# Half of the first norm's modulation columns as products on TensorE, and a new order of the head projections

## What is computed

```python
mod = jax.nn.silu(c) @ w_ada[l] + b_ada[l]            # c: 1 x 1024, w_ada: 1024 x 6144
sh1, sc1, g1, sh2, sc2, g2 = jnp.split(mod, 6, axis=-1)
h = rms_norm(x, g_mix_norm[l]) * (1.0 + sc1[:, None]) + sh1[:, None]
proj = h @ w_in[l]
q_lat, kv_lat, k_pe, qd, kd, vd = jnp.split(proj, SPLITS, axis=-1)
# q, kv from normed q_lat, kv_lat; per-head rms norms; rope on q_pe, k_pe, qd, kd
# two attentions of 8 heads (dense causal; dilated), then
x = x + g1[:, None] * mix                              # mix = both attentions @ w_o
h2 = rms_norm(x, g_ffn_norm[l]) * (1.0 + sc2[:, None]) + sh2[:, None]
x = x + g2[:, None] * (conv-gated ffn of h2)
```

## Time and profile before

| what | value |
|---|---|
| median of 3 runs | 1995.4 us (1995.07 to 1996.27) |
| the profiled execution | 1996.96 us; span from first to last instruction 1995.2 us |
| mean granted TensorE clock | 0.955 |
| PE, DVE, ACT, POOL busy | 93%, 55%, 37%, 14% of the span |
| matmul instructions on PE | 12441 |
| chain that ended last | PE 86%, DVE 6%, ACT 4%, DMA 2% |

### The profile page before, as it was taken

The page is one execution under the profiler, slowest core; times in us unless marked ns, Lnnn a source line. Parts: engine busy times, 40 slices in busy tenths (PEclk is TensorE's granted clock), DMA queues, the critical chain, the costliest instruction groups (busy, mean ns, idle before and its releaser), DMA issues.

```text
span 1995.2 us, 31747 instructions
## 1 busy us (share of the span) xinstructions
PE 1850.2 (93%) x12441; PEld 1631.5 (82%) x12441; DVE 1098.3 (55%) x1742; ACT 744.8 (37%) x1069; POOL 281.0 (14%) x289
## 2 busy tenths in 40 slices
PE   2688779998999999899999999999999899999997
PEld 2565555566888888789999999999999799999995
DVE  5653426556766377754855384433654466654632
ACT  3264436415533233332322263324522454322313
POOL 1001108513000000503004323320000000000000
PEclk8798899989999999989999999998999899999998
DMA  5461320164333332244434462222443123332321
GB/s 182 157 158 45 114 74 12 45 188 86 92 98 90 100 89 88 77 116 123 137 98 99 119 207 70 76 81 92 124 133 99 44 84 93 94 91 81 96 81 46
DMA packets 320275, 198.38 MB, mean 99 GB/s; under 512 B 51159, under 2 KB 303702, under 8 KB 320166
## 3 DMA queue, kind: packets, MB, share of 16 engines
q1 hardware_dynamic: 303520, 154.63, 27.2%
q0 software_dynamic: 9104, 29.02, 4.9%
q10 hardware_dynamic: 7542, 13.23, 1.8%
HBM read 177.23 MB, written 17.24 MB: 97 GB/s over the span
## 4 chain that ended last, share of the span: by engine, by line
PE 86%; DVE 6%; ACT 4%; DMA 2%; issue 2%; SPq 0%; DVEq 0%; POOL 0%; ACTq 0%; POOLq 0%
PE ps L1234 65%; PE ps L1623 3%; PE ps L1682 1%; PE ps L1701 1%; PE ps L1281 1%; DMA ring<-in_w_ada_dram 1%; DVE acol L1842 1%; PE ps L1346 1%; PE ps L1441 1%; PE ps L1476 1%; PE ps L1460 1%; PE ps L1607 1%; PE ps L1603 1%; PE ps L1359 1%; PE ps L1591 1%
## 5 line engine op out<-in xcount | busy, mean ns | idle before, releaser
L1234 PE MATMUL ps<-zhi,whi 128*128 128x264 f32 (+1 forms) x2168 | 685.2, 316 | 23.4 <-DVE zlo L1780 20.2
L1234 PE MATMUL ps<-zhi,wlo 128*128 128x264 f32 (+1 forms) x2168 | 673.8, 311 | 0.0
L1234 PE MATMUL ps<-zlo,whi 128*128 128x264 f32 (+1 forms) x2168 | 672.5, 310 | 0.0
L1234 PEld LDWEIGHTS ps<-zhi,whi 128*128 128x128 f32 x2168 | 415.7, 192 | 56.1 <-issue 24.1
L1770 DVE TENSOR_TENSOR wlo<-stage,whi 128x1024 fp32r<-128x1024 f32 x256 | 327.7, 1282 | 227.3 <-ACT whi L784 221.7
L1234 PEld LDWEIGHTS ps<-zlo,whi 128*128 128x128 f32 x2168 | 416.4, 192 | 22.0 <-issue 2.9
L1234 PEld LDWEIGHTS ps<-zhi,wlo 128*128 128x128 f32 x2168 | 415.6, 192 | 19.3
L784 ACT ACTIVATE whi<-stage 128x1024 fp32r<-128x1024 f32 x256 | 269.2, 1054 | 344.1 <-PE ps L1234 282.0
L1234 PE MATMUL ps<-ghi,whi 128*128 128x264 f32 (+1 forms) x528 | 169.8, 322 | 0.0
L1234 PE MATMUL ps<-ghi,wlo 128*128 128x264 f32 (+1 forms) x528 | 169.7, 321 | 0.0
L1234 PE MATMUL ps<-glo,whi 128*128 128x264 f32 (+1 forms) x528 | 169.6, 321 | 0.0
(11 more groups left out here) (365 smaller groups left out, 2805.7 us busy)
## 6 DMA issues: line engine op xcount, KB each, us to landing
stage<-in_w_up_dram SPq DMA_DIRECT2D x88, 512.0 KB, 3.8
stage<-in_w_in_dram SPq DMA_DIRECT2D x74, 512.0 KB, 4.1
ring<-in_w_ada_dram POOLq DMA_DIRECT2D x32, 512.0 KB, 4.6
stage<-in_w_down_dram SPq DMA_DIRECT2D x32, 512.0 KB, 3.7
adab<-in_w_ada_dram SPq DMA_DIRECT2D x16, 512.0 KB, 7.9
stage<-in_w_down_dram SPq DMA_DIRECT2D x16, 384.0 KB, 3.3
stage<-in_w_o_dram SPq DMA_DIRECT2D x8, 512.0 KB, 3.8
stage<-in_ssm_w_glu_dram SPq DMA_DIRECT2D x8, 512.0 KB, 3.8
```

Of the source, the lines that this page charges most:

```text
L1234: last = pe.matmul(out, w(a, k), x(k, t0, t1), start=(k == 0 and a is whi and x is x_hi), stop=(k == ks - 1 and a is wlo))
```

## The change

- `block` and `block_sums`: DVE multiplies and adds only k = 0 to 3 of each kind (`column`); for k = 4 to 7 PE multiplies the `adab` pieces as stationary operand by the column of `csil`, adding in PSUM, and closes with the ones column on `acol`. Two `acol` sets instead of four.
- DVE, not ACT, copies the transposed x out, one column step of round 0 after each copy. The tables move behind the first products.
- Loads on SP: ada 0 to 3 ahead of `ql` 0 and 1, `ql` 2 ahead of ada 8, `ql` 3 ahead of ada 12. Splits 0 and 1 come before round 1; `first_products` takes three jobs, `ql` 3 becomes a plain job.
- Order of projections: `dk` directly behind `dq`, then `qp`, `kpe`, `kn`, `qn`; groups renumbered. `group_scale` becomes `group_log` and `group_exp` with copy-outs between them.
- Sum 2 moves behind `qn23`, sum 3 behind `dv`, sum 4 from `wo` 4 to `wo` 6, sum 5 behind the norm's statistics; four `asum` tiles.
- The first three splits of `wo` move into attention steps 6 to 8.

The diff, cut to its core (tile addresses, and lists that only follow the new order, are left out):

```diff
-    p.shared("qp", 1, 2, 8)
     p.shared("kn", 1, 4, 8)
-    p.gemm("dk", 4)
     p.shared("qn01", 1, 2, 8)
     p.shared("qn23", 1, 2, 8)
...
             load_unit(sp, 0, unit_views("ql", 0))
             load_unit(sp, 1, unit_views("ql", 1))
-            for u in range(8):
+            for u in range(4, 8):
                 ada_block(u)
             load_unit(sp, 2, unit_views("ql", 2))
+            for u in range(8, 12):
+                ada_block(u)
             load_unit(sp, 3, unit_views("ql", 3))
-            for u in range(8, 16):
+            for u in range(12, 16):
                 ada_block(u)
             sp.dma_start(cst[:, 3 * P:], A["consts"][:, 3 * P:]).then_inc(s_cst2, 16)
             n = 4
-            for name, count in (("kvl", 2), ("dq", 4), ("kpe", 1), ("qp", 1), ("kn", 1), ("dk", 4), ("qn01", 1),
-                                ("qn23", 1), ("mv", 1), ("dv", 4)):
...
-            for k in range(KD):
-                act.wait_ge(xt_mm, k + 1)
-                act.activation(xT[:, k, META:T2], ps[:, 5 + k % 2, :], ACT.Copy).then_inc(xt_done, 1)
+            split_hi(0)
+            split_hi(1)
             act.wait_ge(rs_mm, 1)
             act.activation(rs[:, 0:T1], ps[:, 3, :], ACT.Copy).then_inc(rs_done, 1)
-            for u in range(4):
-                split_hi(u)
+            split_hi(2)
 
             def ahead(name, j):
 
...
-                link(act.activation(sqg[g % 2][:, 0:n, :], ps[:, 4:4 + n, :], ACT.Ln, scale=1.0 / s["w"], bias=small[:, 0:1]))
+                act.activation(sqg[g % 2][:, 0:n, :], ps[:, 4:4 + n, :], ACT.Ln, scale=1.0 / s["w"], bias=small[:, 0:1])\
+                    .then_inc(gln_done, 1)
+
+            def group_exp(g):
+                n = len(GROUPS[g]["tiles"])
+                act.wait_ge(gln_done, g + 1)
                 act.activation(sqg[g % 2][:, 0:n, :], sqg[g % 2][:, 0:n, :], ACT.Exp, scale=-0.5).then_inc(grs_done, 1)
...
             raw("dq", 3)
             act.wait_ge(tab_ready, 2)
             act.activation(tab[:, :, :], tab[:, :, :], ACT.Sin).then_inc(tab_done, 1)
-            raw("kpe", 0)
-            group_scale(0)
-            for j in range(2):
-                raw("qp", j)
-            for j in range(4):
-                raw("kn", j)
-            group_scale(1)
             raw("dk", 0)
             raw("dk", 1)
+            group_log(0)
             raw("dk", 2)
-            group_scale(2)
+            group_exp(0)
             raw("dk", 3)
+            raw("qp", 0)
+            ahead("kpe", 0)
+            group_log(1)
+            raw("qp", 1)
+            group_exp(1)
+            raw("kpe", 0, False)
+            raw("kn", 0)
+            raw("kn", 1)
+            group_log(2)
+            raw("kn", 2)
+            group_exp(2)
+            raw("kn", 3)
             raw("qn01", 0)
-            group_scale(3)
+            group_log(3)
             raw("qn01", 1)
+            group_exp(3)
             raw("qn23", 0)
             raw("qn23", 1)
...
-            for j in range(QB):
-                value_out("mv", j, Vm)
-            group_scale(4)
+            value_out("mv", 0, Vm)
+            value_out("mv", 1, Vm)
+            group_log(4)
+            value_out("mv", 2, Vm)
+            group_exp(4)
+            value_out("mv", 3, Vm)
             for j in range(QB):
                 value_out("dv", j, Vd)
-
-            for u in range(U["wo"], U["wo"] + 3):
-                split_hi(u)
 
...
             for t in range(NS + 5):
+                if 6 <= t < 9:
+                    split_hi(U["wo"] + t - 6)
...
-                pe.wait_ge(acol_done, 2 * r + 2)
+                pe.wait_ge(acol_done, 2 * r + 2)
                 for kind in range(2):
+                    u = 4 * r + 2 * kind + 1
+                    pe.wait_ge(bulk_in[u % 8], 16 * (u // 8 + 1))
                     for i in range(2):
-                        mm = pe.matmul(ps[:, 4 + r, 2 * i + kind:2 * i + kind + 1], acol[2 * r + kind][:, i * P:(i + 1) * P],
-                                       const("ones", n=1), start=True, stop=True)
+                        o = ps[:, 4 + r, 2 * i + kind:2 * i + kind + 1]
+                        for k in range(4):
+                            pe.matmul(o, adab[u % NADA][:, k, i * P:(i + 1) * P], csil[:, 4 + k:5 + k], start=k == 0, stop=False)
+                        mm = pe.matmul(o, acol[2 * (r % 2) + kind][:, i * P:(i + 1) * P], const("ones", n=1),
+                                       start=False, stop=True)
                 mm.then_inc(mod_mm, 1)
...
-                for j in range(4):
+                for j in range(3):
...
             block_sums(0)
+            pe.wait_ge(diag_done, 1)
+            for t in range(QB):
+                mm = pe.matmul(ps[:, 3, t * P:(t + 1) * P], const("ones"), diag[:, t, :], start=True, stop=True)
+            mm.then_inc(rs_mm, 1)
             block_sums(1)
             for k in range(KD):
                 first_products(k)
-                if k in (0, 3):
-                    block_sums(2 + k // 3)
...
                 pe.wait_ge(ada_done, KD * (g - 1))
                 if g > 2:
                     pe.wait_ge(mod_read, g - 2)
+                else:
+                    pe.wait_ge(gsin_done, len(ROTS))
                 for k in range(KD):
-                    mm = pe.matmul(ps[:, 3, k:k + 1], asum[:, k * P:(k + 1) * P], const("ones", n=1), start=True, stop=True)
+                    mm = pe.matmul(ps[:, 3, k:k + 1], asum[g][:, k * P:(k + 1) * P], const("ones", n=1), start=True, stop=True)
                 mm.then_inc(mod_mm, 1)
 
...
@@ -1397,36 +1425,36 @@
             lat_stats(2)
             for j in range(1, 4):
                 z1("dq", j)
-            ada_sums(2)
-            z1("kpe", 0)
+            z1("dk", 0)
             group_rot(0, 0)
+            z1("dk", 1)
             group_stats(0)
+            group_rot(0, 1)
+            z1("dk", 2)
+            z1("dk", 3)
             pe.wait_ge(zlo_done, nbase[3])
             several("qp", 0, 4, lat)
-            group_rot(0, 1)
+            group_rot(1, 0)
+            group_stats(1)
             several("qp", 1, 4, lat)
-            for j in range(4):
-                several("kn", j, 2, kvl)
-                if j == 1:
-                    group_rot(1, 0)
-            group_stats(1)
             group_rot(1, 1)
-            z1("dk", 0)
-            z1("dk", 1)
-            z1("dk", 2)
+            z1("kpe", 0)
+            several("kn", 0, 2, kvl)
+            group_rot(2, 0)
+            several("kn", 1, 2, kvl)
             group_stats(2)
-            z1("dk", 3)
-            ada_sums(3)
+            several("kn", 2, 2, kvl)
+            group_rot(2, 1)
+            several("kn", 3, 2, kvl)
             several("qn01", 0, 4, lat)
-            group_rot(3, 0)
             group_stats(3)
             several("qn01", 1, 4, lat)
-            group_rot(3, 1)
             several("qn23", 0, 4, lat)
             several("qn23", 1, 4, lat)
-            tokens_out("mv", 1, QB, *kvl, 2, 2)
-            group_stats(4)
+            ada_sums(2)
+            tokens_out("mv", 1, QB, *kvl, 2, 2, at={1: 4})
             tokens_out("dv", 4, QB, zx(zhi), zx(zlo), KD, 2)
+            ada_sums(3)
 
 
...
             wait_job_out(pe, J["dv"] + 3)
+            pe.wait_ge(mod_read, 2)
             for t in range(NS + 4):
...
-                if j == 4:
+                if j == 6:
                     ada_sums(4)
+            norm_stats(3)
             ada_sums(5)
-            norm_stats(3)
 
             def ffn(b):
                 f = FFNS[b]
...
                                                   scalar=mod[:, 8 + k:9 + k], in1=col("g_mix", k), op0=ALU.add, op1=ALU.mult))
                     link(dve.tensor_tensor(mod[:, k:k + 1], ps[:, 4 + r, 2 * i + 1:2 * i + 2], col("b_ada", k), ALU.add))
 
+            dve.wait_ge(s_silu, 1)
+            for k in range(KD):
+                dve.wait_ge(xt_mm, k + 1)
+                dve.tensor_copy(xT[:, k, META:T2], ps[:, 5 + k % 2, :]).then_inc(xt_done, 1)
+                column(0, k // 4, k % 4)
+            dve.wait_ge(s_cst, 16)
+            dve.wait_ge(xsq_done, 1)
...
-            dve.wait_ge(s_silu, 1)
-            block(0)
+            split_lo(0)
+            split_lo(1)
             block(1)
-            for u in range(4):
-                split_lo(u)
             dve.wait_ge(rs_done, 1)
...
                 dve.tensor_tensor(HT[:, t0:t0 + n, :], HT[:, t0:t0 + n, :], sqg[g % 2][:, 0:n, :], ALU.mult)\
                    .then_inc(ghead_done, 1)
 
-            for j in range(1, 4):
-                ahead("ql", j)
+            ahead("ql", 1)
+            dve.wait_ge(s_pos, 16)
+            link(dve.tensor_copy(posf[:, :], posi[:, :]))
+            table(0)
+            ahead("ql", 2)
+            ahead("ql", 3)
+            table(1)
             ahead("kvl", 0)
             ada(16)
             ahead("kvl", 1)
-            ada(17)
+            dve.wait_ge(rs_done, 2)
             ahead("dq", 0)
```

(64 more changed lines are left out.)

150 lines of the change are left out of this document (74 added, 76 removed).

## The result

| kernel | median us | runs | ratio to the kernel before | span of the profiled execution |
|---|---|---|---|---|
| before | 1995.24 | 1994.61 to 1996.27 | | 1995.2 |
| changed | 1935.67 | 1932.27 to 1940.15 | 0.9703 [0.9691, 0.9715] | 1930.5 |
| changed, a second time (label `after_again`) | 1935.82 | 1929.56 to 1938.1 | 0.9700 [0.9673, 0.9726] | 1933.9 |

What follows compares the result with a forecast made beforehand. PE, busy 93%, bounds the kernel, so only its waits and slow clock yield time. 18.9 + 42.6 - 2 + 3.4 = 62.9 us off 1996.96 gives 1934.1, by the median 1932.5; range 1917 to 1951.

Steps and rivals of the forecast that it cites:

- Front: Span start to the end of `kvl` 0: less DVE work and reordered loads end it at 86.7 us, gain 18.9.
- Round 1 of the sums: Front: 40 passes on PE at 1.2 GHz take 8.8 us, from 30.7 to 39.5, ending last before the first products.
- Rounds 2 and 3: Front, later sums on PE: three quarters at full clock, then cold, 5.2 us each.
- the tables cost nothing behind `ql`: Front: 10 us of DVE moved beside `ql` 3, `kvl` and `dq`, where DVE has 21 us of work in 40.
- Rival 1: Front: the clock stays at 2.4 GHz through the rounds of sums, giving 1921 us; chance 0.13.
- rival 2: Front: the clock stays at 1.2 GHz through the rounds of sums, giving 1943.3 us; chance 0.14.
- To attention: From the end of `dq` 3 to attention's third step: 160.4 us becomes 117.8, gain 42.6.
- The chain of the ring: Before attention: DVE's ada(24) to (31) end 112.6 us after `dq` 3, so PE idles 5.3 us before sum 3.
- Attention: Three steps get a `wo` split each; bounds 0 and 10.7 us, taken as a loss of 2.
- rival 3: Tight queue: moved splits cost their 10.7 us and ACT slips once by 3.3, 12 more, 1944.5 us; chance 0.13.
- `wo` and the norm: From `wo` through the second norm: last residual 1.1 us earlier, norm's sums no longer behind sum 5, gain 3.4.
- Rival 5: Front: five matmuls accumulating into one PSUM column don't overlap; at 0.45 us extra a pass, 2004 us; chance 0.03.

Runs made afterwards that it cites:

- before_moved: Kernel before with one part of the change alone, the first three `wo` splits moved into attention steps 6 to 8: 1994.87 us, ratio 0.9994.
- best: Changed kernel with ada(24) to (27) ahead of split 23, `wo` splits at attention steps 11, 15, 19 (ACT), 13, 17, 21 (DVE): 1924.25 us.
- ring_early_apart: Changed kernel with ada(24) to (27) ahead of split 23, `wo` splits at attention steps 8, 12, 16 (ACT), 9, 13, 17 (DVE): 1927.50 us.
- splits_apart: Changed kernel with the `wo` splits at attention steps 8, 12, 16 on ACT and 9, 13, 17 on DVE: 1927.43 us, ratio 0.9676.

## Why the prediction was right, point by point

- **Front, 24.1 and 21.8 against 18.9.** DVE ended round 0 at 21.4 us (22.4 forecast) and round 1 at 29.2 (30.7). That is luck: x landed at 11.6 in this execution and not at 12.6, and from there round 0 took 9.8 us, just as forecast. (The terms as written, 12.6 and 8.9, give 21.5; the 22.4 has 0.9 more in it that no term names.) Round 1 of the sums was last and cold, 8.4 us (8.8), and followed PE's own products of diag, which ended at 29.8; PE had no gap from 21.4 on. Rounds 2 and 3 took 4.5 us each, not 5.2, as the clock fell only when they ended. `ql` 3 with `kvl` 0 took 11.4 and not 13.0: I had added 1.8 for a cold start behind the gap, and the clock was full. Round 1's earlier end (1.4), the two rounds (1.3) and this (1.6) carry 4.3 of the 5 us. That the tables cost nothing behind `ql`, and that the loads of rounds 2 and 3 are covered, held: PE waits for `acol` 1.0 us only, in round 0. One profile of each kernel is little here: `before_moved`, with the front of the kernel before, ended `kvl` 0 at 103.9, and nine with the changed front at 84.2 on average, a gain of 20 to 21.
- **The clock: a reading that was wrong.** I read the clock as full from the start of the span to 30.7 us. The traces record it only from its first rise on, and the views print 1.00 for the time before. That rise is at 23.9 us in the kernel before and 17.1 in the changed one (15.6 to 25.4 over the fourteen profiles), and PE's own instructions show it. Twice eight transposes of one form in the kernel before:

```profile
12.63 1.97 PE L1258 MATMUL ps<-cst,xrow 128*128 128x128 f32 x8 [8.41 <-DMA xrow<-in_x_dram]
...
24.64 1.15 PE L1258 MATMUL ps<-cst,xrow 128*128 128x128 f32 x8 [0.23 <-ACT xT L828]
```

  The first eight ran at 1.2 GHz (they started 0.213 us apart, those behind the rise 0.109), though the views print 1.00 there. The Trainium skill ("TensorE: Matmul & The Clock Gate", What's actually happening) takes half rate as the default that activity lifts; these traces agree with it, where I wrote that they did not. The forecast was not hurt, as the clock was full when round 0 began in this execution, at 21.4 us.
- **The clock: what came.** Rival 1 (always full) and rival 2 (always half) are both wrong, and how much of either comes is not fixed from one execution to the next. The same front in `best`, against the rows of the changed kernel above:

```profile
41.00:44.00 3.00, 3.00 (x9) 2.49 (x9) 2.75 (x9) 0.00 (x0) 0.00 (x0) 0.50 0.97 349
44.00:48.00 4.00, 4.00 (x12) 3.10 (x11) 3.76 (x8) 1.38 (x2) 0.00 (x0) 0.61 0.67 224
48.00:52.00 4.00, 4.00 (x31) 3.94 (x29) 2.02 (x5) 0.00 (x0) 0.00 (x0) 0.82 0.01 2
52.00:56.00 4.00, 4.00 (x17) 3.71 (x18) 1.14 (x5) 0.00 (x0) 0.00 (x0) 0.50 0.00 0
```

  Here half of round 2 ran at 1.2 GHz, and by the chain of work the first 18 products took 6.91 us and `ql` 3 with `kvl` 0 12.96, against 5.67 and 11.36: `kvl` 0 ends at 89.2, which is my 86.7 and more. Of the 7.8 us between the two, 1.4 lie ahead of the sums (x landed 1.0 later, at 12.6). Whether this is why the changed kernel's runs spread over 8 us is not shown: the four runs of the kernel before spread over 1.7, but its later sets over 6.9, 6.0 and 3.6, and those of `ring_early_apart`, with the same front, over 1.8.
- **To attention, 43.0 and 42.1 against 42.6.** The large terms held. The sum as written is 117.4 and not 117.8, and PE reached the end of `dv` 3 at 108.7 us behind `dq` 3, not 107.3, which the wait for the ring hid. Rotation (0,1) costs nothing (the 1.1 us of `rtp` that are left stand at rotation (2,1)), `mv` 3 to `dv` 0 leaves 1.5 of `wlo` (1.7 forecast). The chain of the ring ended 112.1 us behind `dq` 3 (112.6); sum 3 waited 3.4, ran cold for 3.6, and was read. It is what is late next, as forecast. The three landings at its end took 4.96, 3.98 and 3.94 us; by the 3.2 that I worked out from the Trainium skill ("DMA: Bandwidth & Descriptors", Anatomy of one DMA) the wait would have nearly gone, and it didn't.
- **Attention, -8.5 against -2: the wrong step.** The bounds were 0 and 10.7, and I took a value near the low end "by DVE's share of idle time". That share is spread over 32 steps, while the splits stood in three, one behind the other, with DVE waiting for ACT. The nearer row was that of DVE's splits on the page of the kernel before, where nearly all of the idle time ahead of them ends on ACT's split:

```profile
L1770 DVE TENSOR_TENSOR wlo<-stage,whi 128x1024 fp32r<-128x1024 f32 x256 | 327.7, 1282 | 227.3 <-ACT whi L784 221.7
```

  From it each split should have been priced at 1.05 + 1.23 and a wait, 2.3 or more, three times over. The first half of rival 3 came true within the range, and by another way than its price: no weight block landed late, and the 8.5 are the three splits, 6.9, and waits. `splits_apart` and `best` show that the place, and not the amount, was at fault.
- **`wo` and the norm, 5.3 and 2.9 against 3.4.** Right within the scatter of this stretch; that sum 5's move is the cause is not settled.
- **Sum.** The front's surplus and attention's loss nearly cancel, so that the total came this near is in part luck. 1932.5 was forecast and 1935.7 measured; the profiled execution at 1932.27 is the fastest of the four.

## What to carry to other kernels

A high/low split by two engines is a chain: spread the units over a pipelined loop, with the two halves in different steps, each where its engine waits for something else anyway, and don't size such work by an engine's mean idle share. When an engine is made to wait for a last transfer, the price is the wait and the half clock behind it; look for idle time of the consumer that lies earlier in its own queue. A gain or a loss upstream of another wait is worth only what exceeds that wait.

## What the runs showed of the hardware

- One-column matmuls kept PE busy all the time (8.00 of 8 us), and the clock fell under them all the same, to 1.2 GHz at 23.9 us in the changed kernel; with wide products among them (one fp32 of 384 columns, or two fp32r of 512, behind each ten passes) it fell as well, at 24.1 and 23.2.
- The granted clock that the views print ahead of its first recorded rise is no measurement: eight transposes took 1.97 us under a printed 1.00, and 1.15 behind the rise.
- An fp32 product of 128x384 took 0.73 us at 2.4 GHz, more than three times an fp32r product of 128x512 (0.232).
- The same front, instruction for instruction, ended between 81.4 and 89.2 us in nine profiles; in the two extremes compared above most of the difference lies in stretches whose granted clock differs (6.91 against 5.67 us for the first 18 products, 12.96 against 11.36 for `ql` 3 with `kvl` 0).
- Five matmuls that accumulate into one PSUM column follow each other without extra cost: 8.4/40 = 0.21 us a pass at 1.2 GHz and 4.5/40 = 0.11 at 2.4, as the single ones in the earlier trace rows. Rival 5 is out.
